# Identity products around the opening's clock drop, and a 3 MB table written in another stage

## The reference, cut to what matters

```python
c_act = jax.nn.silu(c)
for i in range(DEPTH):
    mod = c_act @ mod_w[i] + mod_b[i]                 # 9 vectors of 1024
    sh1, sc1, g1, sh2, sc2, g2, sh3, sc3, g3 = jnp.split(mod, 9, axis=-1)
    h = modulate(rmsnorm(x, norm_g[i, 0]), sh1, sc1)  # h * (1 + scale) + shift
    x = x + 0.5 * g1 * swiglu(h, ffn_w13[i, 0], ffn_w2[i, 0])
    h = modulate(rmsnorm(x, norm_g[i, 1]), sh2, sc2)
    m = pool_ssd_mixer(h, ...) if i == 0 else mla_mixer(h, ...)   # state space, latent attention
    x = x + g2 * m
    ...                                               # a second swiglu
```

## Time and profile before

| what | value |
|---|---|
| median of three runs | 1822.02 us (1819.73 to 1822.78) |
| the profiled execution, its own time | 1821.97 us |
| its span | 1820.2 us |
| PE busy | 1733.0 us (95%) |
| DVE busy | 1250.7 us (69%) |
| ACT busy | 877.8 us (48%) |
| mean granted PE clock | 0.995 of 2.4 GHz |
| DMA | 352.78 MB, mean 194 GB/s |

### The profile page before, as it was taken

One profiled execution on the slowest core, in us unless ns is written; L12 is line 12 of the kernel. 1 busy time (PEld: TensorE's weight loads), 2 busy tenths in 40 slices (PEclk: granted clock), 3 DMA queues, 4 the chain that ended last, 5 costly groups with the idle time before them and its releaser, 6 DMA issues.

```text
span 1820.2 us, 33142 instructions
## 1 busy us (share of the span) xinstructions
PE 1733.0 (95%) x12198; PEld 1588.6 (87%) x12198; DVE 1250.7 (69%) x2120; ACT 877.8 (48%) x1411; POOL 74.3 (4%) x119
## 2 busy tenths in 40 slices
PE   6999999999999999999999999999999999999998
PEld 5899988888999889998778999899877789879997
DVE  6887878568777877766556555589798565555554
ACT  2444457534444434445565444545355655554443
POOL 2000011200000100000000000100000000000000
PEclk9999999999999999999999999999999999999999
DMA  9888847657988688864433655354532154435551
GB/s 352 304 304 295 285 143 201 142 197 245 303 296 289 193 314 291 290 203 133 134 93 92 229 187 184 118 174 147 161 93 76 47 185 163 138 118 196 184 186 67
DMA packets 123657, 352.78 MB, mean 194 GB/s; under 512 B 9850, under 2 KB 52874, under 8 KB 114224
## 3 DMA queue, kind: packets, MB, share of 16 engines
q1 hardware_dynamic: 108128, 262.18, 44.5%
q10 hardware_dynamic: 12432, 78.65, 12.6%
q0 software_dynamic: 3008, 10.74, 1.7%
HBM read 347.31 MB, written 4.22 MB: 193 GB/s over the span
## 4 chain that ended last, share of the span: by engine, by line
PE 72%; DVE 15%; ACT 6%; issue 4%; DMA 2%; POOL 1%; ACTq 0%; DVEq 0%; POOLq 0%
PE ps L779 65%; DVE w_lo L189 3%; DVE arena L2669 2%; ACT w_hi L183 2%; PE ps L354 1%; DVE arena L344 1%; DMA resid<-in_x 1%; DVE resid L1205 1%; DMA arena<-in_mod_w 1%; PE ps L647 1%; DVE act_s L2989 1%; PE ps L3058 1%; PE ps L2976 0%; DVE act_s L3023 0%; DVE tmp L1202 0%
## 5 line engine op out<-in xcount | busy, mean ns | idle before, releaser
L779 PE MATMUL ps<-t_hi,w_hi 128*128 128x256 f32 (+1 forms) x2616 | 748.4, 286 | 12.5 <-DVE t_lo L708 5.4
L779 PE MATMUL ps<-t_lo,w_hi 128*128 128x256 f32 (+1 forms) x2616 | 740.8, 283 | 0.0
L779 PE MATMUL ps<-t_hi,w_lo 128*128 128x256 f32 (+1 forms) x2616 | 740.6, 283 | 0.0
L779 PEld LDWEIGHTS ps<-t_hi,w_hi 128*128 128x128 f32 (+1 forms) x2616 | 500.2, 191 | 28.5 <-issue 14.5
L779 PEld LDWEIGHTS ps<-t_lo,w_hi 128*128 128x128 f32 (+1 forms) x2616 | 500.5, 191 | 2.1
L779 PEld LDWEIGHTS ps<-t_hi,w_lo 128*128 128x128 f32 (+1 forms) x2616 | 500.4, 191 | 0.2
L1066 DVE TENSOR_TENSOR w_lo<-raw,w_hi 128x1024 fp32r<-128x1024 f32 x258 | 313.8, 1224 | 157.2 <-ACT w_hi L1055 157.1
L189 DVE TENSOR_TENSOR w_lo<-raw,w_hi 128x1024 fp32r<-128x1024 f32 x240 | 288.9, 1223 | 151.7 <-ACT w_hi L183 151.6
L1055 ACT ACTIVATE w_hi<-raw 128x1024 fp32r<-128x1024 f32 x258 | 269.4, 1054 | 174.9 <-PE ps L779 174.5
L183 ACT ACTIVATE w_hi<-raw 128x1024 fp32r<-128x1024 f32 x240 | 248.6, 1053 | 147.4 <-PE ps L779 105.6
L779 PE MATMUL ps<-w_hi,g_hi 128*128 128x512 f32 x440 | 176.2, 400 | 5.9 <-DVE g_lo L1097 5.7
(11 more groups left out here) (349 smaller groups left out, 1670.9 us busy)
## 6 DMA issues: line engine op xcount, KB each, us to landing
raw<-in_stream SPq DMA_DIRECT2D x498, 512.0 KB, 4.3
arena<-in_mod_w ACTq DMA_DIRECT2D x72, 1024.0 KB, 6.9
grow<-gate_scratch POOLq DMA_DIRECT2D x6, 512.0 KB, 8.5
u_scratch<-u_keep ACTq DMA_DIRECT2D x1, 3072.0 KB, 35.1
arena<-u_scratch POOLq DMA_DIRECT2D x8, 256.0 KB, 3.2
small<-in_small POOLq DMA_DIRECT2D x1, 1368.0 KB, 11.0
resid<-in_x POOLq DMA_DIRECT2D x1, 1024.0 KB, 18.7
arena<-in_mem POOLq DMA_DIRECT2D x1, 1024.0 KB, 5.3
```

The costliest lines, as they stand in the source:

```text
L779: last = TE.matmul(out, lhs, rhs, start=start and i == 0, stop=stop and i == 2)
```

## The change: what it does

```diff
@@ opening, the block of PE with the four modulation turns
             mod_turn(pe, 1, first=True)
             keep_busy(ps[4], 8)
             mod_turn(pe, 2, first=True)
-            keep_busy(ps[4], 6)
+            keep_busy(ps[4], 12)
             mod_turn(pe, 3, first=True)
@@ transpose_tile in turn
                     prior = kt - 2
+                    if kt == 4 and done:
+                        keep_busy(ps[2], 3)
                     if kt >= 4 and not by_tokens:
@@ after states()
         states()
-        @block.scalar
-        def _(act):
-            act.dma_start(u_dram, u_keep[:, :].unsqueeze(1)
-                          .to_broadcast([HEADS, P, 384])).then_inc(scratch.sem, scratch.up(16))
@@ after ffn(2, ...), ahead of the attention helper and of the latent attention's norm_x
         ffn(2, N_MOD - PRE - 2 * FG - 1, PRE + 2 * FG + 1, (mod_at(1, 2), 0.5))
+        @block.scalar
+        def _(act):
+            act.dma_start(u_dram, u_keep[:, :].unsqueeze(1)
+                          .to_broadcast([HEADS, P, 384])).then_inc(scratch.sem, scratch.up(16))
```

## The result

The kernel after takes 1834.73 us (median of 5 runs), the kernel before in the same session 1822.02 us (5 runs, 1819.26 to 1822.89). The ratio is 1.007, with an interval of 1.0058 to 1.0082: some 12.7 us slower, where 1822.4 was forecast. One run of 2118.5 us, at a mean granted clock of 0.753, is left out of the ratio. The profiled execution took 1833.92 us (span 1832.1), 11.95 more than that of before. Lines behind 635 stand two higher in the kernel after (L779 is now L781, L2096 is L2098).

What follows compares the result with a forecast made beforehand. PE was taken to bound most of the span, with its clock at 1.2 GHz in the opening; 1821.97 - 1.75 (opening) + 0 (mixer) + 2.2 (stall at the latent attention) = 1822.4 us, range 1819.3 to 1826.2.

Steps and rivals of the forecast that it cites:

- The step that failed: Latent attention: loads served again 24.7 us after the table's issue, block 244 landing at 851.05, PE stalling 2.2 us.
- the forecast's 3.5: Latent attention: time in us taken for the first load, block 244, to land once loads are served again.
- rival 3: Latent attention: SP's loads get nothing until the table is through, PE stalls 10.3 us; 1830.5 us, chance 0.10.
- Rival 1: Latent attention: both queues take turns from the start, so the table is hidden; 1820.2 us, chance 0.25.
- POOL's root: Latent attention: step queued behind block 244's split and the mean, ahead of PE's spreading; slack 0.92 us.
- Gain 0: State-space mixer: moving the table's write away removes no wait; gain 0, upper bound 0.69 us.
- Six products: Opening, ahead of the fourth turn: hidden by the wait for DVE's sums; cost 0, upper bound 1.8 us.
- rival 4: Opening: products run at 1.2 GHz and delay the fourth turn by up to 1.8 us; 1824 us or a little above, chance 0.05.
- Three products: Opening, ahead of tile 4: cost 0, 0.2 us late at the slow pace; clock expected at 2.4 GHz over 44 to 51 us.
- Gain 1.75: Opening: filled idle stretches keep PE's clock up, gate product begins 1.75 us earlier; bounds 0 and 2.1 us.

Runs made afterwards that it cites:

- e5: Kernel before with the table's write moved to the latent attention and the table written a second time right behind it; 1844.34 us, ratio 1.0119.
- e7: Kernel before with the table's write moved behind ACT's copy of the narrow product of the latent attention, amid the block loads; 1830.72 us, ratio 1.0047.
- e2: Kernel before with only the table's write moved to the end of the ffn ahead of the latent attention; 1837.65 us, ratio 1.0077.
- e6: Kernel before with the table's write moved to the latent attention as two DMAs of half rows, 4096 packets of 768 B; 1834.99 us, ratio 1.007.
- e8: Kernel before with eight of sixteen heads of the table written at the old place, eight at the new one; 1837.13 us, ratio 1.0082.
- e11: Kernel before with the whole table issued by POOL on its own queue, ahead of the latent attention; 1840.65 us, ratio 1.009.
- e3: Kernel before with only the six more products ahead of the fourth turn; 1822.79 us, ratio 1.0008.
- e1: Kernel before with only the nine products of the opening, the table's write left in the state-space mixer; 1824.4 us, ratio 1.0009.
- e4: Kernel before with only the three products ahead of tile 4; 1821.71 us, ratio 1.0006.
- e9: Kernel before with 96 of 128 copies of the table at the old place, 32 amid the latent attention's block loads; 1824.56 us, ratio 1.0006.

## Why the prediction was wrong, step by step

**The step that failed** reads: "At the old place SP's loads were served again from 338.3, which is 24.7 us after the issue at 313.61. The same from 822.85 is 847.55." I tied the end of the standstill to the table's issue. The runs tie it to the issue of the load that waits. In the kernel before the load was asked for at 323.7 and served from 338.3, 14.6 us later; in the kernel after it was asked for at 838.16, with its packets, but for a few, from about 852.5 on, 14.3 later. The table had been issued 10 us ahead of the one load, and 17 us ahead of the other. Block 244 landed at 855.9, not at 851.05 less the 1.39 by which all was earlier, so 6.2 us late. With the right rule the sum was to be had from rows 8 and 9 alone: asked for at 839.55, served 14.6 later at 854.15, with the forecast's 3.5 landing at 857.65, a stall of 857.65 - 847.93 - 0.92 = 8.8 us and 1829.0 us in all. The number that was missed is the time from the load's issue to its first packet, and both readings had one row to go by. I took the one without asking from what else the time could be counted. Nor does the rule by the load's issue hold for every load: the one asked for 0.40 us behind the table at the old place had its first packet after 3.9 us, and why it got through isn't known.

**Which rival it was.** The size is that of rival 3 (1830.5), and the table's end lies within 1 us of the block's landing; but its mechanism is refuted by e5, and by e7, where the load's first packet came at 853.32 and the table's end at 871.88. That the number came near is luck. It was a fourth case between forecast and rival 3, with a price from the same rows, and I had given it no chance. Rival 1 is refuted by the 7 packets.

**The clock behind the stall** was not in the sum. PE stalls for 7.07 us and then runs at 0.50 for 6.5 us, which costs 2.25. With the 2.4 us ahead of the stall and the 1.6 us at 977.5 that is 6.25 us more than the corrected sum has; the stall is 8.8 - 7.07 = 1.7 shorter, and 1829.0 + 6.25 - 1.7 is 1833.5, for 1833.92 measured. The stall by its parts: 8.8, less 0.35 as the block landed at 855.9 and not at 857.65 - 1.39, plus 1.0 for POOL's root, less the 2.4 that came first and took up part of the wait, is 7.05.

**POOL's root** I took at its 0.70 us; it took 1.69. It does so where DVE's next split runs beside it, as at 858.27 above. In e2, e6 and e8, where the second block had landed too and was being split, it took 1.65 to 1.69; in e5 and e11, where DVE is idle after the mean, 0.70 and 0.72. The kernel before has the longer time as well, at another place: 1.67 us for an operation of the same shape at 1422.26, beside DVE's split of 1422.08.

**"Gain 0" in the mixer** is nearly right: the markers are 0.6 us earlier behind it (+0.3 before 305, -0.35 at 370 us). The issue's 0.69 us on ACT was given as its upper bound.

**Six products, "Cost 0"**: right in e3 at 2.92 us for the 24 records, wrong in after and in e1 at 4.46 and 4.93. The bound of 1.8 us was the right price (the turn 2.2 and 1.8 us late). The chance of 0.05 was not: the late rise of the clock on which rival 4 rests is there in five of fourteen profiles (42.03 us or later), and two of the three with the six products had it.

**Three products, cost 0, and the clock holds**: the cost is borne out in e4, where tile 4's transposes follow as before. The clock reads 1.00 there, but it had risen at 38.80, and the old opening holds it then too. For the forecast that the clock would hold, rows 3 were little to go by: they are for another stage, and the idle time within that window is 3.40 - 1.94 = 1.46 us, while the 1.9 of rows 3 counts what came before it as well. **Gain 1.75** was a little too much: 1.2 to 1.5 us, and only in those executions in which the clock would have fallen.

## What to carry to other kernels

A long DMA of small packets delays the loads that are issued from 1 us behind it on, on the same DMA engines, whichever queue it comes from, and the wait, some 14 us here, counts from that load's issue. So look for the place where the next load is needed at least 20 us after it is asked for, as in the mixer, or cut the DMA along a dimension that keeps all 16 DMA engines, so that it is through before. When a gap in a trace is to be moved in time, write down every event from which it could be counted, and price each. A column that has no record behind it can still show a number, so check it against the pace of the instructions. An effect of the clock that one profile shows has to be looked for in several before work is put on it.

## What the runs showed of the hardware

- A load asked for 1.1 to 24 us behind the issue of the table, with over 60 packets per DMA engine left, got its first packet after 12.8 to 15.4 us (before, after, e1, e2, e3, e4, e5, e7), in which 54 to 62 packets of 1536 B per DMA engine passed. In rows of the table it was 68 of 768 B in e6 and 62 of 1536 B in e11, and in e9 the 32 that were left. One asked for 0.40 us behind the whole table got its first packet after 3.0 to 4.0 us (before, e1, e3, e4). Before the result I quoted the rule that DMA engines take turns between queues, packet by packet, as speaking against rows 8. What stands beside it in the Trainium skill ("DMA: Bandwidth & Descriptors", Queues, rings and completion order) I left out: a packet in that sense is up to 64 descriptors, and typically 9 to 17. If the rows of the table are its descriptors, 64 x 0.21 = 13.5 us, an estimate, comes close to what was measured. Turns between such blocks would not by themselves give the same wait to loads that come at different times, 10 and 17 us behind the table's issue. What in the DMA engine makes the count is left open.
- After this wait the queues share: in e7 from 857.3 to 867 us q1 got 564 packets through and q10 579.
- A second DMA of 2048 packets issued right behind the first held ACT for 9.86 us (e5) and 7.65 us (e6); a first one takes 0.69 us.
- In the opening the clock rose from 1.2 to 2.4 GHz at 36.2 to 42.7 us, at another time in each of the fourteen profiles; the same 24 records took 2.92 us behind an early rise (e3) and 4.93 across a late one (e1). It fell again only in the five old openings in which it had risen by 37.3 us.
- POOL's 128x2 product took 0.70 us with DVE idle and 1.65 to 1.69 us beside DVE's 128x1024 split.
